# Three pairs of split weight buffers in place of four

## The chip, the cores and the metric

The kernel runs as one program on one core of a Trainium2 chip. The metric is the device time of one execution in microseconds (us), lower is better. The profile's times count from the start of the span, which is the part of the execution in which the engines work.

## The reference

Two blocks of a network run one after the other on 256 tokens of width 1024, batch 1, in float32. The first has a retention layer, a gated embedding, shared keys and values with compressed blocks, a sparse attention layer and a second gated embedding:

```python
def first_block(...):
    h = retention_layer(x, ret_norm, ret_w_in, ret_gn, ret_w_out)   # 4 heads, q k 256, v 512 wide, gate, out
    h = h + sigmoid(rmsnorm(h, g0) @ ple_w_gate0) * (p0 @ ple_w_emb0)
    shared = nsa_shared_kv(h, ...)      # rmsnorm(h) @ kv_w: 6 parts of 512; two of them compressed
    h = nsa_layer(h, ..., *shared)      # 16 heads in 4 groups: compressed, selected and window branch
    h = h + sigmoid(rmsnorm(h, g1) @ ple_w_gate1) * (p1 @ ple_w_emb1)
    return rmsnorm(h, final_norm)

def compress_blocks(a, pe, w1, w2):     # windows of 32 tokens, stride 16: 15 windows for each group
    return gelu((blocks + pe) @ w1) @ w2          # w1 is 4096 x 256

def nsa_layer(...):
    q, gate, bgate = split(rmsnorm(h, g) @ w_in)
    o = sigmoid(bgate)[0] * o_compressed + sigmoid(bgate)[1] * o_selected + sigmoid(bgate)[2] * o_window
    return h + (silu(gate) * o) @ w_out
```

With 256 tokens there are four selection blocks and the window is 512, so that the selected and the window branch are both plain causal attention. The second block takes that output as x:

```python
def second_block(x, ...):
    ua, va, za, qh, kh, vh, zb, ga, gb = split(x @ w_in)            # 9 parts of 1024
    ya = gelu(ua) * (spatial mix of layer_norm(gelu(va))) * silu(za)
    o  = softmax(q1 k1) v - lam * softmax(q2 k2) v                   # 8 heads, rotary, causal, then rms_norm
    yb = o * silu(zb)
    merged = sigmoid(ga) * (ya @ w_branch_a) + sigmoid(gb) * (yb @ w_branch_b)
    ple = sigmoid(x @ w_ple_gate) * (p @ w_ple)
    return layer_norm(2 ** 0.25 * x + merged @ w_out + ple)
```

## The kernel before

Activations stay on the chip. What streams in is the weights, 145 chunks of them, numbered 0 to 144 in the order of their first use (`plan.chunks`). A full chunk is 1 MB: four tiles of 128 rows by 512 columns (for the compression's first matrix, eight tiles by 256 columns), 2048 float32 values in each partition. Ten chunks are half as large and one is smaller still.

Each product of float32 numbers is made of three products in the type fp32r: a number is split in a high part (the number cast to fp32r) and a low part (the number less the high part), and TensorE adds high x high, high x low and low x high. For the weights this works as follows, for every chunk c:

- SyncE issues the transfer into `raw[c % 3]` (line 664). From chunk 3 on it first waits until chunk c - 3 has been split (`lo_done`, line 661).
- ScalarE makes the high part, `whi[c % SPLIT_SLOTS]`, a cast of 128 x 2048 (line 773). It waits for the transfer, and from chunk SPLIT_SLOTS on for the use of the chunk that had the buffer before (line 772).
- VectorE makes the low part, `wlo[c % SPLIT_SLOTS]`, a subtraction (line 1168). It waits for the high part.
- TensorE waits for `lo_done`, does the chunk's matmuls, and counts `chunk_used` up at the last one (lines 1703 to 1758).

Both ScalarE and VectorE have a helper `split_until(n)`, which makes all parts up to chunk n - 1 in order; each engine's whole program is written in one order, and an engine does nothing behind a wait until that wait is met. The order in which the parts are made is set by the calls of the helper:

```python
def before_block(name):
    split_until(plan.upto[name] + AHEAD)     # AHEAD = 3
    block_wait(act, name)
```

`plan.upto[name]` is the number of chunks that TensorE's order has introduced up to and with the block or the misc step `name`. So before ScalarE or VectorE waits for the result of block `name`, whose last chunk is `upto - 1`, it makes its parts of all chunks up to `upto + 2`. `before_misc` does the same for the small matmuls and transposes in between; for the transposes of a norm the look-ahead is 1 or 2 instead of 3. In some places only `split_until(... + AHEAD)` stands, ahead of a wait of another kind: ahead of the sigmoids of a gated embedding (line 878) and of the residual's adds on VectorE (line 1238), which wait for each of the two row tiles by itself.

TensorE's order is written out by hand in `tensor_order`. A block is a product with 512 columns of weights, in one to four chunks. Blocks alternate between two pairs of banks (`acc`); a block waits until its pair has been read. Two layouts occur: "nat" has the tokens in the rows of the result, with the activations as the stationary operand (lines 1718 to 1735), "tr" has them in its columns, with the weights stationary (lines 1742 to 1744). Small steps ("misc") go round four banks (`mps`): each waits until the step four before it has been read. These are the norms' transposes and all others (line 1761), the scores (lines 1841 to 1851), the transposes of the probabilities (1859, 1862) and the products with the values (1873, 1876) in the sparse attention, and the steps of the differential attention (1901, 1919 to 1921).

The order around the places that matter:

- Retention output: blocks `ret_out0`, `ret_out1` (chunks 26 to 33), then `emb0_0` and `emb0_1` (34, 35, half size), then the transposes of the norm `ple0`, then `ple0_0` and `ple0_1` (36 to 39). VectorE adds the residual (line 1242), and scales the rows (line 1209).
- `ple0_1`, `emb1_0`, `emb1_1` (40, 41), norm `kv`, then `kc`, `vc`, `ks` (42 to 47), the compression `cmp_k` (48 to 51), `kw` and `vs` (52 to 55), `cmp_v` (56 to 59), `vw` (60, 61), the first queries (62, 63) and the branch gate `nsa_b` (64; ScalarE's sigmoid is line 962, TensorE's transposes of it line 1816).
- Sparse attention, four groups of four chunks (65 to 80). In group 1 these are 69 to 72: scores of the first query tile, 69, compressed scores and scores of the second tile, 70, transposes, 71, values, transposes, 72, values. VectorE reads the scores in lines 1404 and 1418, weighs the value product in line 1445; ScalarE copies the transposes in line 994.
- The rest of `nsa_out` (81 to 86), `emb2_0` (87), norm `ple1`, `ple1_0` and `ple1_1` (88 to 91), `emb2_1` (92), norm `fin`, `ple2` (93 to 96), and the projections of the second block (97 to 120).
- Differential attention with `zb`, `ga`, `wa`, `gb` between its steps (121 to 136), then `wb0` first chunk (137), `ob` of the last heads, `wb1` first chunk (138), transposes of `ob`, gating (line 1650), `wb0` and `wb1` second chunks (139, 140), merge (line 1625) and `wo` (141 to 144).

Of the kernel before, what the change touches and what calls it, by code (L numbers as in the profile page):

```python
# [43 lines left out]


RAW_SLOTS = 3
SPLIT_SLOTS = 4
AHEAD = 3
CH = 2048
MISC = 4  # L50
# [325 lines left out]
def build(nc, w, consts, ret_consts, out):  # L376
# [5 lines left out]
    with ExitStack() as ctx:  # L382
        def sb(name, shape, dt=F32):
            return ctx.enter_context(nc.sbuf_tensor(name, shape, dt))
# [5 lines left out]
        raw = [sb(f"raw{i}", [P, CH]) for i in range(RAW_SLOTS)]  # L390
        whi = [sb(f"whi{i}", [P, CH], F32R) for i in range(SPLIT_SLOTS)]
        wlo = [sb(f"wlo{i}", [P, CH], F32R) for i in range(SPLIT_SLOTS)]

# [365 lines left out]
        def _(act):  # L759
# [3 lines left out]
            def split_until(n):  # L763

                while done[0] < min(n, len(plan.chunks)):
# [3 lines left out]
                    act.wait_ge(raw_in[c % RAW_SLOTS], 16 * (c // RAW_SLOTS + 1))  # L769
                    if c >= SPLIT_SLOTS:  # L770

                        act.wait_ge(chunk_used, plan.used_up[c - SPLIT_SLOTS])
                    nc.scalar.activation(whi[c % SPLIT_SLOTS][:, 0:size], raw[c % RAW_SLOTS][:, 0:size],  # L773
                                         ACT.Copy).then_inc(hi_done, 1)
# [378 lines left out]
        def _(dve):  # L1153
# [7 lines left out]
            def split_until(n):  # L1161

                while done[0] < min(n, len(plan.chunks)):
# [3 lines left out]
                    dve.wait_ge(hi_done, c + 1)  # L1167
                    nc.vector.tensor_tensor(wlo[c % SPLIT_SLOTS][:, 0:size], raw[c % RAW_SLOTS][:, 0:size],  # L1168
                                            whi[c % SPLIT_SLOTS][:, 0:size].bitcast(F32),
# [808 lines left out]
```

## Time and profile before

| | before |
|---|---|
| median of 3 runs | 916.99 us (916.43 to 917.31) |
| the profiled execution | 917.05 us, its span 915.0 us |
| TensorE matmuls busy | 888.4 us (97%) |
| VectorE busy | 569.2 us (62%) |
| ScalarE busy | 482.7 us (53%) |
| GpSimd busy | 37.1 us (4%) |
| moved by DMA | 154.95 MB, mean 169 GB/s |
| mean granted clock of TensorE | 0.994 |

A line of the timeline has the start in us, the duration in us, the engine, the line in the kernel, the operation, what it writes and reads with the shapes, and how many instructions are merged in it. In brackets stand the engine's idle time before it and what ended that idle time. PE is TensorE's matmul queue, DVE is VectorE, ACT is ScalarE. Matmuls overlap, so one of 390 ns can follow another by 230 ns.

### The profile page before, as it was taken

How to read it: one execution, taken by the hardware profiler on the slowest of the kernel's cores; microseconds unless marked ns; L12 is line 12 of the kernel's file. 1: busy time of each engine (PE TensorE's matmuls, PEld its weight loads, DVE VectorE, ACT ScalarE, POOL GpSimd, SP SyncE). 2: the span in 40 equal slices, each digit the busy share in tenths (PEclk: the TensorE clock that was granted, in tenths of full speed). 3: DMA queues.
4: the chain of work that ended last, by engine and by line, in shares of the span. 5: the costliest groups of instructions: out<-in, count | busy, mean ns of one | idle time of the engine just before them, and what ended most of it. 6: DMA issues, size and time to landing. Idle time of an engine off the chain costs nothing.

```text
span 915.0 us, 13668 instructions
## 1 busy us (share of the span) xinstructions
PE 888.4 (97%) x5662; PEld 786.1 (86%) x5662; DVE 569.2 (62%) x831; ACT 482.7 (53%) x709; POOL 37.1 (4%) x48
## 2 busy tenths in 40 slices
PE   5999999999999999999999999899999999999995
PEld 5998898888799988878878687788998889999994
DVE  4885565546685675544646346786559548567675
ACT  5433433327655766665757436644434448756630
POOL 1000000000100000000000002100020000000002
PEclk9999999999999999999999999999999999999998
DMA  8755544543767875324142356465556526454421
GB/s 296 269 191 182 183 134 144 196 140 113 231 200 251 278 233 165 126 93 127 58 138 75 131 185 208 158 237 184 190 177 232 184 92 212 157 185 152 132 86 46
DMA packets 81325, 154.95 MB, mean 169 GB/s; under 512 B 3761, under 2 KB 11953, under 8 KB 81265
## 3 DMA queue, kind: packets, MB, share of 16 engines
q1 hardware_dynamic: 79760, 149.23, 48.9%
q0 software_dynamic: 1504, 4.85, 1.8%
q8 instruction: 45, 0.74, 0.3%
q14 instruction: 16, 0.12, 0.0%
HBM read 153.03 MB, written 1.05 MB: 168 GB/s over the span
## 4 chain that ended last, share of the span: by engine, by line
PE 90%; ACT 3%; DVE 3%; DMA 2%; issue 1%; POOL 0%; SPq 0%; POOLq 0%; DVEq 0%; ACTq 0%
PE acc L1742 14%; PE acc L1743 13%; PE acc L1744 13%; PE acc L1733 7%; PE acc L1734 7%; PE acc L1735 7%; PE acc L1720 5%; PE acc L1718 5%; PE acc L1719 5%; PE misc L1873 2%; DMA raw<-in_ret_w_in_dram 2%; PE misc L1761 2%; PE misc L1846 2%; ACT whi L773 2%; DVE wlo L1168 1%; PE misc L1862 1%
## 5 line engine op out<-in xcount | busy, mean ns | idle before, releaser
L1168 DVE TENSOR_TENSOR wlo<-raw,whi 128x2048 fp32r<-128x2048 f32 (+1 forms) x145 | 317.4, 2204 | 166.8 <-ACT whi L773 166.2
L773 ACT ACTIVATE whi<-raw 128x2048 fp32r<-128x2048 f32 (+1 forms) x145 | 266.6, 1845 | 162.1 <-PE acc L1735 81.1
L1742 PE MATMUL acc<-xhiA,whi 128*128 128x256 f32 x576 | 165.2, 287 | 0.5 <-DVE wlo L1168 0.5
L1743 PE MATMUL acc<-xloA,whi 128*128 128x256 f32 x576 | 163.6, 284 | 0.0
L1744 PE MATMUL acc<-xhiA,wlo 128*128 128x256 f32 x576 | 163.4, 284 | 0.0
L1742 PEld LDWEIGHTS acc<-xhiA,whi 128*128 128x128 f32 x576 | 110.9, 193 | 2.9 <-issue 2.2
L1743 PEld LDWEIGHTS acc<-xloA,whi 128*128 128x128 f32 x576 | 110.9, 193 | 0.0
L1744 PEld LDWEIGHTS acc<-xhiA,wlo 128*128 128x128 f32 x576 | 110.9, 193 | 0.0
L1742 PE MATMUL acc<-xhiC,whi 128*128 128x256 f32 x320 | 93.6, 292 | 0.3 <-DVE xloC L1192 0.3
L1744 PE MATMUL acc<-xhiC,wlo 128*128 128x256 f32 x320 | 90.7, 283 | 0.0
L1743 PE MATMUL acc<-xloC,whi 128*128 128x256 f32 x320 | 90.7, 283 | 0.0
L1733 PE MATMUL acc<-whi,xhiA 128*128 128x512 f32 x160 | 64.3, 402 | 0.7 <-DVE xloA L1227 0.7
L1742 PEld LDWEIGHTS acc<-xhiC,whi 128*128 128x128 f32 x320 | 61.4, 192 | 1.5 <-issue 1.0
L1734 PE MATMUL acc<-wlo,xhiA 128*128 128x512 f32 x160 | 62.4, 390 | 0.0
L1735 PE MATMUL acc<-whi,xloA 128*128 128x512 f32 x160 | 62.4, 390 | 0.0
L1743 PEld LDWEIGHTS acc<-xloC,whi 128*128 128x128 f32 x320 | 61.5, 192 | 1.0 <-issue 1.0
L1744 PEld LDWEIGHTS acc<-xhiC,wlo 128*128 128x128 f32 x320 | 61.4, 192 | 0.0
L1742 PE MATMUL acc<-xhiB,whi 128*128 128x256 f32 x192 | 54.9, 286 | 0.9 <-DVE xloB L1227 0.9
L1743 PE MATMUL acc<-xloB,whi 128*128 128x256 f32 x192 | 54.4, 283 | 0.0
L1744 PE MATMUL acc<-xhiB,wlo 128*128 128x256 f32 x192 | 54.4, 283 | 0.0
L1720 PE MATMUL acc<-whi,xloA 128*128 128x512 f32 x128 | 49.9, 390 | 0.0
L1718 PE MATMUL acc<-whi,xhiA 128*128 128x512 f32 x128 | 49.9, 390 | 0.0
(253 smaller groups left out, 1579.6 us busy)
## 6 DMA issues: line engine op xcount, KB each, us to landing
raw<-in_w_in_dram SPq DMA_DIRECT2D x36, 1024.0 KB, 5.1
raw<-in_ret_w_in_dram SPq DMA_DIRECT2D x22, 1024.0 KB, 5.2
raw<-in_nsa_w_in_dram SPq DMA_DIRECT2D x16, 1024.0 KB, 5.2
raw<-in_kv_w_dram SPq DMA_DIRECT2D x12, 1024.0 KB, 5.3
raw<-in_ret_w_out_dram SPq DMA_DIRECT2D x8, 1024.0 KB, 5.1
raw<-in_ple_w_gate_dram SPq DMA_DIRECT2D x8, 1024.0 KB, 5.2
raw<-in_nsa_w_out_dram SPq DMA_DIRECT2D x8, 1024.0 KB, 5.1
raw<-in_cmp_w_k_dram SPq DMA_DIRECT2D x4, 1024.0 KB, 7.2
```

What stands on the lines that cost most here:

```text
L773: nc.scalar.activation(whi[c % SPLIT_SLOTS][:, 0:size], raw[c % RAW_SLOTS][:, 0:size], ACT.Copy).then_inc(hi_done, 1)
L1168: nc.vector.tensor_tensor(wlo[c % SPLIT_SLOTS][:, 0:size], raw[c % RAW_SLOTS][:, 0:size], whi[c % SPLIT_SLOTS][:, 0:size].bitcast(F32), AL ...
L1718: nc.tensor.matmul(o, xh, hi[:, j], start=first and j == 0, stop=False)
L1719: nc.tensor.matmul(o, xh, lo[:, j], start=False, stop=False)
L1720: ins = nc.tensor.matmul(o, xl, hi[:, j], start=False, stop=(j == len(ks) - 1))
L1733: nc.tensor.matmul(o, xh, hi[:, j, off:off + cols], start=start, stop=False)
L1734: nc.tensor.matmul(o, xh, lo[:, j, off:off + cols], start=False, stop=False)
L1735: ins = nc.tensor.matmul(o, xl, hi[:, j, off:off + cols], start=False, stop=stop)
L1742: nc.tensor.matmul(o, wh, xh, start=s0, stop=False, skip_group_check=True)
L1743: nc.tensor.matmul(o, wh, xl, start=False, stop=False, skip_group_check=True)
L1744: ins = nc.tensor.matmul(o, wl, xh, start=False, stop=stop, skip_group_check=True)
L1761: ins = nc.tensor.transpose(dst[:, i * P:i * P + P], s, ident)
```

## The change

The number of buffer pairs for the split weights goes from four to three. The names `whi[3]` and `wlo[3]` go away, chunk c uses the pair c % 3, and ScalarE's wait of line 772 is for the use of chunk c - 3, from chunk 3 on. The buffers for the raw weights stay three and the look-ahead stays 3. Each pair takes 16 KB in every partition.

```diff
@@ -44,7 +44,7 @@
 RAW_SLOTS = 3
-SPLIT_SLOTS = 4
+SPLIT_SLOTS = 3
 AHEAD = 3
 CH = 2048
 MISC = 4
```

The lines that it governs, unchanged themselves:

```python
whi = [sb(f"whi{i}", [P, CH], F32R) for i in range(SPLIT_SLOTS)]
wlo = [sb(f"wlo{i}", [P, CH], F32R) for i in range(SPLIT_SLOTS)]
...
if c >= SPLIT_SLOTS:
    act.wait_ge(chunk_used, plan.used_up[c - SPLIT_SLOTS])
```

## Rows read from the trace of the kernel before

**Rows 1.** The page: busy time of the engines; the groups of instructions by line.
```profile
PE 888.4 (97%) x5662; PEld 786.1 (86%) x5662; DVE 569.2 (62%) x831; ACT 482.7 (53%) x709; POOL 37.1 (4%) x48
...
L1168 DVE TENSOR_TENSOR wlo<-raw,whi 128x2048 fp32r<-128x2048 f32 (+1 forms) x145 | 317.4, 2204 | 166.8 <-ACT whi L773 166.2
```

**Rows 2.** Timeline, 190 to 221 us: the end of the retention output and its norm.
```profile
191.01 1.92 ACT L773 ACTIVATE whi<-raw 128x2048 fp32r<-128x2048 f32 x1 [3.52 <-PE acc L1735]
...
207.33 1.92 ACT L773 ACTIVATE whi<-raw 128x2048 fp32r<-128x2048 f32 x1 [4.38 <-PE acc L1735]
...
212.51 0.39 PE L1718 MATMUL acc<-whi,phi 128*128 128x512 f32 x1
...
215.34 0.75 DVE L1209 TENSOR_SCALAR arena<-h,rstd 128x1024 f32<-128x1024 f32 x1 [0.67 <-POOL rstd L681]
...
220.57 0.47 PE L1733 MATMUL acc<-whi,xhiA 128*128 128x512 f32 x1 [0.70 <-DVE xloA L1227]
```

**Rows 3.** Timeline, 237 to 251 us: the gated embedding and the norm before kc.
```profile
237.25 1.92 ACT L773 ACTIVATE whi<-raw 128x2048 fp32r<-128x2048 f32 x1 [1.71 <-PE acc L1735]
...
242.63 0.60 ACT L881 ACTIVATE arena<-acc 128x512 f32<-128x512 f32 x1 [2.12 <-PE acc L1720]
...
250.75 0.35 PE L1742 MATMUL acc<-xhiB,whi 128*128 128x256 f32 x1 [0.92 <-DVE xloB L1227]
```

**Rows 4.** Timeline of TensorE: after the norm ple1, and the norm fin.
```profile
556.93 0.47 PE L1733 MATMUL acc<-whi,xhiC 128*128 128x512 f32 x1 [0.93 <-DVE xloC L1227]
...
584.26 1.09 PE L1761 MATMUL misc<-cbuf,arena 128*128 128x128 f32 x4 [2.56 <-DVE arena L1209]
```

**Rows 5.** Windows: stretch, length, busy us of each engine, granted clock, DMA.
```profile
584.00:586.00 2.00, 1.74 (x9) 1.77 (x10) 0.11 (x1) 0.62 (x2) 0.76 (x2) 0.52 0.52 147
586.00:587.50 1.50, 1.50 (x9) 1.50 (x9) 1.16 (x3) 1.47 (x5) 0.00 (x0) 0.51 0.98 281
```

**Rows 6.** Timeline, 288 to 353 us: compression and branch gate.
```profile
288.50 6.90 DVE L1168 TENSOR_TENSOR wlo<-raw,whi 128x2048 fp32r<-128x2048 f32 x3 [4.38 <-ACT whi L773]
...
322.65 0.39 PE L1755 MATMUL acc<-whi,xloA 128*124 128x256 f32 x1 [0.69 <-DVE wlo L1168]
...
352.87 0.29 PE L1816 MATMUL misc<-cbuf,arena 48*128 48x48 f32 x2 [0.16 <-ACT arena L962]
```

**Rows 7.** Timeline, 402 to 425 us: group 1 of the sparse attention.
```profile
402.83 0.96 PE L1851 MATMUL misc<-arena 128*128 128x15 f32 x8
404.59 2.74 PE L1846 MATMUL misc<-arena 128*128 128x512 f32 x6
405.53 0.17 DVE L1404 CUSTOM_DVE_ANT_0 arena<-misc,cbuf 128x15 f32<-128x15 f32 x1
...
419.97 0.59 PE L1873 MATMUL misc<-arena 128*128 128x512 f32 x1
...
422.94 0.69 DVE L1445 TENSOR_TENSOR arena<-misc,arena 128x512 f32<-128x512 f32 x1 [1.28 <-PE misc L1876]
...
424.83 0.61 PE L1859 MATMUL misc<-cbuf,arena 128*15 128x128 f32 x4
```

**Rows 8.** Timeline, 753 to 757 us and 870 to 884 us: differential attention and tail.
```profile
753.08 4.50 DVE L1168 TENSOR_TENSOR wlo<-raw,whi 128x2048 fp32r<-128x2048 f32 x2
756.50 0.28 PE L1742 MATMUL acc<-xhiA,whi 128*128 128x256 f32 x1
...
870.96 0.60 PE L1761 MATMUL misc<-cbuf,arena 128*128 128x128 f32 x4
...
872.52 0.74 DVE L1650 SCALAR_TENSOR_TENSOR arena<-misc,small,arena 128x512 f32<-128x512 f32 x1
...
874.71 0.38 PE L1742 MATMUL acc<-xhiC,whi 128*128 128x256 f32 x1 [0.27 <-DVE xloC L1192]
...
877.97 1.40 DVE L1625 TENSOR_TENSOR arena<-arena,acc 128x512 f32<-128x512 f32 x2
...
881.83 1.22 DVE L1192 TENSOR_TENSOR xloB<-arena,xhiB 128x1024 fp32r<-128x1024 f32 x1 [1.20 <-ACT xhiB L786]
```

## The prediction

> **What bounds the kernel now.** I read the busy shares first. TensorE works in 97% of the span [rows 1], so it is the bound, and every new wait in its order adds to the time unless an old one gives way to it. The second view was the groups by line: a split on VectorE takes 2.2 us on average, 145 of them, and of VectorE's idle time 166 us ended when ScalarE's half of a split was done [rows 1]. So both engines have room, but much of it lies in front of a split, in program order, ahead of other work. The third was TensorE's order of time with its waits: after the start there are few gaps, the largest being 2.56, 0.93, 0.92, 0.70 and 0.69 us, 6.2 us for all that I show [rows 2 to 4, 6, 8]. They lie where a normalisation, a compression or a gate has to come back from ScalarE and VectorE. Those places already have no slack. The question is what the edit does there.
>
> In steady flow, ScalarE's half of chunk 33 starts at 191.01, which is when chunk 29 has been used. With 1.92 us of ScalarE and VectorE's 2.2 us [rows 1] it is full at 195.2. TensorE wants the chunk when chunk 32 is used, at 207.2 (ScalarE's next wait for it ended at 207.33) [rows 2]. The pair is full 12 us early.
>
> **The change.** It issues, removes and adds no instruction and no byte; what changes is one wait. ScalarE's half of chunk c waits for the use of chunk c-3 instead of c-4. A full chunk takes TensorE 5.3 us there (207.2 to 212.5, where the next block's first matmul is at 212.51), and somewhat more in the other layout. Chunk 33's split would start 5.3 us later, and be full some 6.6 us early. A plain split therefore stays hidden, in nearly the whole kernel. That costs nothing by itself, and no DMA is late: the transfer of c+3 still starts when VectorE has split c, and has a whole chunk's matmuls to land.
>
> The cost comes from what stands behind the split. The look-ahead stays at three, so before it waits for a block or a misc step, ScalarE first has to split the third chunk after it, and that now needs the very last chunk before the awaited step, where it needed the one before that. Both engines run in order, so everything behind is late by what is left of a chunk, plus 1.9 us of ScalarE and 2.3 of VectorE. I followed each engine's order through the kernel chunk by chunk. Where the lateness is absorbed I name the cover.
>
> *Retention, and the last block's projections.* The copies, the rotary products and the group norms come 2 to 5 us later. Their readers are a whole chunk away. 0 us; without that cover up to 4 us for each.
>
> *Norm after the retention output.* The residual's last column half stands behind the split of chunk 36. That split began at 207.33, at the end of chunk 32; now it needs chunk 33, and 212.5. The residual add behind it and the normed rows at 215.34 (second tile) move 5.3 us. TensorE had its next full chunk at 220.57, after other cover of about 2 us had run out [rows 2]. With ScalarE's extra split in the way as well, I take +4.1 us. Bounds: 3 (only the rows are late) to 5.4.
>
> *Norm before the kv projections.* Split 42 moves from 237.25 to 242.6, past both sigmoids. The second began at 242.63 when the chunk ended. TensorE already waited 0.92 us for this norm's result at 250.75 [rows 3], so nothing covers it: +5.4. The norm after the attention output (0.93 us waited, chunk 88 at 556.93) and the one before the last block (2.56 us waited) have the same two forms [rows 4]: +5.4 each. Bounds for each of the three: 4 to 6.
>
> *Compression.* The four chunks of each compression take TensorE less time each than VectorE's half of a split, so the lead is eaten. VectorE splits chunks 51 to 53 back to back from 288.50 (2.3 us each), and TensorE starts 52 the moment it is full, at 293.1; it waits 0.69 us for chunk 59 at 322.65 [rows 6]. This run begins later, since split 50 now needs chunk 47 and a copy of a key block moves in between; by the engines' orders I get 52 full at 295.1: +2.05 (an estimate). The second compression adds +2.15, by way of a copy behind split 58, which now waits for chunk 55. Bounds together: 2 to 7.
>
> *Branch gate.* It already ends TensorE's 0.16 us wait at 352.87 [rows 6]. Split 66 now stands ahead of the copy before it: 1.9 us later, +1.95. Bounds: 0 to 2.1.
>
> *Attention, four groups alike.* First, chunk 69 ends at about 403.0, where TensorE turns to the compressed scores (402.83). VectorE's first operation on these is at 405.53, behind split 72. This can't begin before 403.05 now, and is full at 403.05 + 1.9 + 2.3 = 407.25: +1.7. The fourth of the group's second scores needs this bank back; three of them take 2.74 us from 404.59, so it starts at 406.4. It would get the bank, four small operations later, at 407.8: +1.4. Second, split 74 must now wait for chunk 71, at 420.1 (TensorE turns to the weighted values at 419.97). It is full at 420.2 + 1.9 + 2.3 = 424.4, so the product of 422.94 moves 1.5 us, and with it ScalarE's copies, which free a bank for the last transpose at 424.83 [rows 7]: +1.5. In all 4 x 2.9 = 11.6. Bounds: 2 to 16.
>
> *Differential attention.* At its start VectorE splits chunks 122 and 123 at 753.08, behind an exponential of ScalarE; so 122 is full at 755.3, and wanted at 756.50 [rows 8]. ScalarE now stops for split 123 until chunk 120 is used, and is 2.1 us late; 1.2 are covered: +0.9, say 1.0 with the semaphore's way. After that ScalarE and VectorE run 2 to 4 us behind, but by their reader's order they are a chunk ahead: 0, bounds 0 to 4.
>
> *Tail.* The last head's outputs are needed at once. Split 141 had been long asked for; now it needs chunk 138, which ends at 871.1 (the transposes at 870.96), itself 1.5 us later because an earlier copy on ScalarE is late. 871.1 + 1.5 + 1.9 + 2.3 = 876.8, in place of 872.52, for the gating behind it: +4.4 at TensorE's wait of 874.71. Chunk 139 then ends at 882.2, where it ended just before 877.97; split 142 waits for it and takes 4.2; the merge at 877.97 starts at 886.5. From there to TensorE's next chunk (its operand ready at 881.83 + 1.22 = 883.05) it is 5.4 us: 891.8 instead of 883.4 [rows 8]. The tail in all: +8.3. Bounds: 4 to 10. No splits are left after it.
>
> Sum: 4.1 + 3 x 5.4 + 4.2 + 1.95 + 11.6 + 1.0 + 8.3 = 47.4 us.
>
> **The clock.** After the 2.56 us gap the granted clock was 0.52 from 584 to 586 and 0.51 on to 587.5 [rows 4, 5], the lower level (1.2 GHz), 3.3 us in all; most of that lay behind the waits of the norm anyway. Three norms get gaps of 4 to 6 us, and the tail 2.6 and 3.5. I add 0.4 us for each of the three, and 1.3 for the tail: 2.5. Bounds 0 to 13 (eight gaps over 2 us at 1.6 each, the half-speed share of those 3.3 us).
>
> The Trainium skill (page TensorE: Matmul & The Clock Gate, section HAM oscillation — how this bites in real kernels) says that a wait between bursts of matmuls can send the clock back to its lower level, so that the next burst starts slow; the trace agrees at 584.
>
> The sum is made against the profiled execution: span 915.0, 917.05 us in all. 917.05 + 47.4 + 2.5 = 967.0; the median of the runs, 916.99, lies 0.06 lower, so I say 967.
>
> **Rivals.**
> R1, nothing is seen: three pairs are enough. For it speaks that a split is full 6.5 us early still, and that over 160 us of VectorE's time are idle. It turns on one thing: if the work behind a split (residual adds, gating, bank releases) had over 5.4 us before its reader, all lateness would vanish. Against it stand TensorE's present waits at these places [rows 3, 4, 8]. Its time: 917. The Trainium skill (page Trainium Kernel Development and Optimization, section Best Practices) advises double buffering to overlap transfers with computing, and three is more than double; by that rule this one would hold.
> R2, only late splits cost: the compressions and chunk 122, 5 us, and the first norm's; the norms' other chains go on as before because the engines find time in between. 917 + 5 to 10: 925. Against it: the engines don't reorder.
> R3, the same and more: every gap over 2 us brings the lower clock for a whole 3.3 us on the path (+10), or lateness adds up from head to head in the differential attention (+4 for some): 975 to 990.
> R4, half: the bank waits in attention don't arise, since the banks come back earlier than I read, and the tail costs 4: 967 - 11.6 - 4.3 = 951.
>
> **How the numbers follow.** Forecast 0.62, with a range of its own of 958 to 975; R4 0.14; R3 0.12; R2 0.06; R1 0.06. The range of 8 in 10 takes in R4 and the lower part of R3: 946 to 979. About 0.2% (1.8 us) can be told from no change. Faster: 0.01, since nothing is removed that anyone waits for; the same 0.06; slower 0.93.
>
> **What would show it.** TensorE busy about the same in us, some 92% of the span; its idle up by some 47 us, with waits of 4 to 8 us before the norms' transposes at the four norms (releaser: VectorE's normed rows), 1.4 and 1.5 us in each attention group, and two in the tail before the gating's low half and before the first chunk of the output projection. ScalarE's idle before splits goes up, released by TensorE. Wrong would be: no gaps at the norms (R1), a stall in steady flow with the low half of a split as its releaser, or a slower matmul.

## The result and the profile after

The changed kernel takes 976.52 us, the median of four runs (974.56 to 979.8); the kernel before took 916.71 in four runs beside them (916.12 to 917.31). The ratio is 1.0656, with a 95% interval of 1.0624 to 1.0688: slower, by 59.8 us. The forecast was 967.0 (946 to 979), so the sign, the cause and the range held; its likeliest case, 958 to 975, ended 1.5 us too low, and the range held by the part that it had taken in from the rival R3. The profiled execution took 975.62 us, of which the span is 973.6, with a mean granted clock of 0.973 (0.994 before).

The page of the changed kernel: busy time by engine, the granted clock in 40 slices, the chain that ended last by engine, and the two groups of splits (busy us, mean ns of one, idle time ahead of them and what ended it).

```profile
PE 907.9 (93%) x5662; PEld 799.1 (82%) x5662; DVE 569.8 (59%) x831; ACT 486.2 (50%) x709; POOL 37.4 (4%) x48
...
PEclk9999999999899998999999998899999999999979
...
PE 83%; ACT 7%; DVE 5%; issue 3%; DMA 1%; POOL 1%; SPq 0%; POOLq 0%; DVEq 0%; ACTq 0%
...
L1168 DVE TENSOR_TENSOR wlo<-raw,whi 128x2048 fp32r<-128x2048 f32 (+1 forms) x145 | 319.3, 2206 | 298.5 <-ACT whi L773 297.8
L773 ACT ACTIVATE whi<-raw 128x2048 fp32r<-128x2048 f32 (+1 forms) x145 | 267.2, 1845 | 330.2 <-PE acc L1744 141.1
```

Beside [rows 1]: the counts are the same, and VectorE and ScalarE work as long as before. A split costs VectorE 2206 ns in place of 2204, so no split got slower. VectorE's idle time in front of its splits went from 166.8 to 298.5 us, and ScalarE's from 162.1 to 330.2, most of it ended by TensorE. The two engines do the same work and stand longer ahead of it. In the chain that ended last TensorE's share went from 90% to 83%, ScalarE's from 3% to 7%, VectorE's from 3% to 5%. TensorE's own row is the surprise: 907.9 us busy for the same 5662 matmuls, 19.5 more than before. Busy time that grows without a matmul more points to a lower clock, and the digits 8 and 7 in the row of the clock say in which slices.

TensorE's timeline after the change has these long waits (in brackets: the idle time and what ended it):

```profile
218.56 0.80 PE L1718 MATMUL acc<-whi,phi 128*128 128x512 f32 x1 [3.82 <-DVE h L1242]
225.37 0.47 PE L1733 MATMUL acc<-whi,xhiA 128*128 128x512 f32 x1 [0.70 <-DVE xloA L1227]
...
257.84 3.65 PE L1761 MATMUL misc<-cbuf,arena 128*128 128x128 f32 x16 [4.42 <-DVE arena L1209]
...
337.31 0.44 PE L1755 MATMUL acc<-whi,xloA 128*124 128x256 f32 x1 [2.18 <-DVE wlo L1168]
...
370.91 0.29 PE L1816 MATMUL misc<-cbuf,arena 48*128 48x48 f32 x2 [2.01 <-ACT arena L962]
...
431.98 1.13 PE L1846 MATMUL misc<-arena 128*128 128x512 f32 x2 [1.29 <-DVE small L1404]
...
450.90 0.66 PE L1862 MATMUL misc<-cbuf,arena 128*128 128x128 f32 x4 [0.76 <-DVE arena L1445]
452.05 0.61 PE L1859 MATMUL misc<-cbuf,arena 128*15 128x128 f32 x4 [0.49 <-ACT arena L994]
...
592.70 3.65 PE L1761 MATMUL misc<-cbuf,arena 128*128 128x128 f32 x16 [5.84 <-DVE arena L1209]
...
628.89 3.65 PE L1761 MATMUL misc<-cbuf,arena 128*128 128x128 f32 x16 [7.73 <-DVE arena L1209]
...
925.34 0.58 PE L1742 MATMUL acc<-xhiC,whi 128*128 128x256 f32 x1 [2.75 <-DVE xloC L1192]
940.31 0.47 PE L1733 MATMUL acc<-whi,xhiB 128*128 128x512 f32 x1 [3.42 <-DVE xloB L1192]
```

The releasers are normed rows, a residual add, a gate, a bank release and an operand: results that came late. Behind the opening only two kinds of wait end with a split itself, those of the compressions and of chunk 122. How a late result arises is plain on VectorE, here at the end of the retention output; it answers to [rows 2]:

```profile
212.12 1.92 ACT L773 ACTIVATE whi<-raw 128x2048 fp32r<-128x2048 f32 x1 [4.38 <-PE acc L1720]
...
214.06 2.29 DVE L1168 TENSOR_TENSOR wlo<-raw,whi 128x2048 fp32r<-128x2048 f32 x1 [5.07 <-ACT whi L773]
...
217.82 0.68 DVE L1242 TENSOR_TENSOR h<-h,acc 128x512 f32<-128x512 f32 x1
...
220.12 0.75 DVE L1209 TENSOR_SCALAR arena<-h,rstd 128x1024 f32<-128x1024 f32 x1 [0.68 <-POOL rstd L681]
```

The same instructions in the kernel before:

```profile
209.28 2.29 DVE L1168 TENSOR_TENSOR wlo<-raw,whi 128x2048 fp32r<-128x2048 f32 x1 [5.07 <-ACT whi L773]
...
213.04 0.68 DVE L1242 TENSOR_TENSOR h<-h,acc 128x512 f32<-128x512 f32 x1
```

VectorE stood idle for 5.07 us in front of this split before as well. What changed is when the wait is met: the split starts at 214.06 in place of 209.28, since ScalarE's half now waits until chunk 33 is used and not chunk 32. The last add comes at 217.82 in place of 213.04, and the normed rows at 220.12, where they came at 215.34.

A table of where the 58.6 us between the spans (973.6 less 915.0) arise. Each number is the growth, from one place to the next, of the difference between the start of a chunk in that kernel and in the kernel before, in one profiled execution each. Two experiments stand beside it, told below. (The first norm's row ends at the start of chunk 41. 0.5 of it, in all three columns, arises there, where `emb1_1` waits 0.31 us for banks that ScalarE's sigmoid of line 881 frees; by its cause it belongs to the gated embedding and so to the row below.)

| place | forecast | changed | changed, with fillers | four pairs, look-ahead 4 |
|---|---|---|---|---|
| start | 0 | -0.65 | -0.4 | -0.1 |
| norm after the retention output | 4.1 | 5.9 | 4.6 | 6.1 |
| norm before `kc` | 5.4 | 5.7 | 4.7 | 5.8 |
| compression 1 | 2.05 | 1.8 | 1.8 | -0.1 |
| compression 2 | 2.15 | 3.4 | 1.9 | -0.5 |
| branch gate | 1.95 | 5.1 | 1.8 | 1.9 |
| attention, four groups | 11.6 | 11.95 | 11.9 | 11.95 |
| norm `ple1` | 5.4 | 6.3 | 5.4 | 5.8 |
| norm `fin` | 5.4 | 6.3 | 4.5 | 6.0 |
| chunk 122 | 1.0 | 0.9 | 0.9 | 0.0 |
| differential attention | 0 | 0.25 | 0.2 | 0.25 |
| tail | 8.3 | 11.7 | 7.8 | 10.5 |
| clock, told by itself | 2.5 | in the above | | in the above |
| sum | 49.9 | 58.6 | 45.1 | 47.5 |

### The profile page after: what moved, and what is told of

Same layout as the page of the kernel before. It is cut to its first block, busy times and chain, and to the rows that moved or that the text cites. A ratio compares the mean times of both kernels' runs of the same rounds, so it can differ in the third digit from the quotient of the medians.

```text
span 973.6 us, 13669 instructions
## 1 busy us (share of the span) xinstructions
PE 907.9 (93%) x5662; PEld 799.1 (82%) x5662; DVE 569.8 (59%) x831; ACT 486.2 (50%) x709; POOL 37.4 (4%) x48
## 4 chain that ended last, share of the span: by engine, by line
PE 83%; ACT 7%; DVE 5%; issue 3%; DMA 1%; POOL 1%; SPq 0%; POOLq 0%; DVEq 0%; ACTq 0%
PE acc L1742 13%; PE acc L1743 13%; PE acc L1744 13%; PE acc L1733 7%; PE acc L1734 6%; PE acc L1735 6%; PE acc L1718 5%; PE acc L1720 5%; PE acc L1719 5%; ACT whi L773 4%; DVE wlo L1168 3%; PE misc L1761 2%; DMA raw<-in_ret_w_in_dram 1%; PE misc L1873 1%; PE misc L1841 1%
## 5 line engine op out<-in xcount | busy, mean ns | idle before, releaser
L1168 DVE TENSOR_TENSOR wlo<-raw,whi 128x2048 fp32r<-128x2048 f32 (+1 forms) x145 | 319.3, 2206 | 298.5 <-ACT whi L773 297.8
L773 ACT ACTIVATE whi<-raw 128x2048 fp32r<-128x2048 f32 (+1 forms) x145 | 267.2, 1845 | 330.2 <-PE acc L1744 141.1
L1733 PE MATMUL acc<-whi,xhiA 128*128 128x512 f32 x160 | 64.7, 405 | 0.7 <-DVE xloA L1227 0.7
L1735 PE MATMUL acc<-whi,xloA 128*128 128x512 f32 x160 | 62.6, 391 | 0.0
L1761 PE MATMUL misc<-cbuf,arena 128*128 128x128 f32 x184 | 31.1, 325 | 27.5 <-DVE arena L1209 27.3
L1761 PEld LDWEIGHTS misc<-cbuf,arena 128*128 128x128 f32 x184 | 26.9, 171 | 29.8 <-issue 29.1
```

The costliest lines, as they stand in the source:

```text
L1733: nc.tensor.matmul(o, xh, hi[:, j, off:off + cols], start=start, stop=False)
L1735: ins = nc.tensor.matmul(o, xl, hi[:, j, off:off + cols], start=False, stop=stop)
L1761: ins = nc.tensor.transpose(dst[:, i * P:i * P + P], s, ident)
```

## The experiments

The theory, T1: the pair that is missing hurts by the order of the programs. A split that is asked for `AHEAD` chunks early waits for the use of the chunk `SPLIT_SLOTS` before it; with both at three, that is the last chunk of the very block whose result stands behind the split. Rivals: T2, the pairs themselves are too few to keep TensorE fed; T3, the raw buffers come free later, and the transfers arrive late; and for the 10 us beyond the waits, that the clock is not what costs them.

Each ratio below is to the kernel before, measured beside the experiment; its medians there are 916.2 to 916.8.

**Three pairs, look-ahead 2** (`s3_a2`) and **four pairs, look-ahead 2** (`s4_a2`).

```diff
-AHEAD = 3
+AHEAD = 2
```

> Three pairs, look-ahead 2 in place of 3. T1 (order: the cost is that a split whose wait is for the last chunk of the awaited block stands ahead of the reads of that block) expects nearly the time of the kernel before, 917 to 930 us, say 924: the split ahead of a read then needs the last chunk but one again, and only the places with short chunks (the compressions, chunk 122) still have too little lead. T2 (shortage: three pairs hold too little, whatever the order) expects 976 us or more, since splits are asked for later still. T3 (transfers start late) expects 970 to 980.

> Four pairs as before, look-ahead 2. T1 expects the kernel before or a little less, 910 to 918 us, say 914: the splits ahead of the norms' reads then wait for a chunk that has long been used, so that a part of the 5 us of gaps at the four norms goes. T2 expects 917 to 925, since pairs are filled later. T3 expects 917 to 920.

Measured: 930.08 (929.33 to 931.01) with three pairs, ratio 1.0150 (1.0135 to 1.0165), and 929.99 (929.1 to 930.25) with four, ratio 1.0147 (1.0132 to 1.0162). One constant gives 46 of the 60 us back with three pairs, and at look-ahead 2 a fourth pair makes no difference that can be told. T2 falls. But the times that T1 had named, 924 and 914, were missed by 6 and by 16: a shorter look-ahead has a price of its own. Of the 12.7 in the span 5.7 are at the compressions, where the lead is eaten, and 7.5 at chunk 121. VectorE's and TensorE's timelines of four pairs, look-ahead 2:

```profile
758.79 0.16 DVE L1567 TENSOR_TENSOR small<-small 128x1 f32<-128x1 f32 x1 [11.27 <-ACT small L1087]
758.99 0.15 DVE L1568 TENSOR_SCALAR small<-small 128x1 f32<-128x1 f32 x1
759.17 2.29 DVE L1168 TENSOR_TENSOR wlo<-raw,whi 128x2048 fp32r<-128x2048 f32 x1
```

```profile
761.57 0.55 PE L1742 MATMUL acc<-xhiA,whi 128*128 128x256 f32 x1 [4.76 <-issue]
```

VectorE waits 11.27 us for an exponential of ScalarE, and the low half of chunk 121 stands behind that wait. With look-ahead 3 it was made before it. "issue" as the releaser is a place where the page does not name the cause; VectorE's split that ends at 761.46 does.

**Three pairs, look-ahead 2, and chunk 121 split before that wait** (`s3_a2_lam`). One line is added on VectorE:

```diff
+                split_until(plan.upto["vh1"] + 1)
                 dve.wait_ge(lam_done, 1)
```

> Three pairs, look-ahead 2, and VectorE makes its half of chunk 121 before it waits for the exponential of lambda instead of behind it. The order theory puts 6.6 us of the 13 that look-ahead 2 still costs on that one place (TensorE waits 4.8 us for chunk 121 and runs half of it slowly), so 930 - 6.6 = 923.5 us, 921 to 926. If the 13 us were a general lack of lead, nothing would change: 929 to 931.

Measured: 923.71 (921.86 to 924.39), ratio 1.0072 (1.0054 to 1.0089). The wait of 4.76 is gone, and three pairs now cost 0.7%. Of what is left, 6.3 in the span, 5.6 are at the compressions.

**Four pairs, look-ahead 4** (`s4_a4`). The reverse test: no buffer is taken away, but look-ahead and pairs are equal again.

```diff
-AHEAD = 3
+AHEAD = 4
```

> Four pairs as before, look-ahead 4 in place of 3: as many buffers as before, but the split ahead of a read again needs the last chunk of the awaited block. T1 expects the slowdown of the change nearly whole: 955 to 977 us, say 968, less than 976 only where the second chunk of lead helps (compressions, chunk 122). T2 expects 910 to 917, since nothing is taken away and pairs are filled earlier. T3 expects 917.

Measured: 966.48 (963.42 to 969.36), ratio 1.0546 (1.0517 to 1.0576). The kernel before, with nothing removed, loses 50 us at the same places with the same waits (last column of the table). What it doesn't show are the compressions (-0.6 for both) and chunk 122 (0). These are what the missing pair adds at look-ahead 3, 4.6 us without the clock. From its timeline of TensorE:

```profile
219.09 0.79 PE L1718 MATMUL acc<-whi,phi 128*128 128x512 f32 x1 [3.82 <-DVE h L1242]
...
258.55 3.65 PE L1761 MATMUL misc<-cbuf,arena 128*128 128x128 f32 x16 [4.43 <-DVE arena L1209]
...
365.88 0.30 PE L1816 MATMUL misc<-cbuf,arena 48*128 48x48 f32 x2 [2.01 <-ACT arena L962]
...
584.48 3.44 PE L1761 MATMUL misc<-cbuf,arena 128*128 128x128 f32 x16 [5.84 <-DVE arena L1209]
620.17 3.65 PE L1761 MATMUL misc<-cbuf,arena 128*128 128x128 f32 x16 [7.74 <-DVE arena L1209]
```

Waits of 3.82, 4.43, 2.01, 5.84 and 7.74, where the changed kernel has 3.82, 4.42, 2.01, 5.84 and 7.73.

**Five raw buffers** (`s3_raw5`), against T3.

```diff
-RAW_SLOTS = 3
-SPLIT_SLOTS = 4
+RAW_SLOTS = 5
+SPLIT_SLOTS = 3
```

> Three pairs, look-ahead 3 as in the changed kernel, but five raw buffers in place of three, so that every weight transfer may start two chunks earlier than now. It tells the order of the programs (T1) from the transfers (T3: with three pairs the raw buffers come free later and the weights arrive late). T1: the first halves wait for a pair, not for a raw buffer, and a second half still frees its raw buffer in the same order; time 974 to 979, the same waits of TensorE at the same places (3.8 before the second gated embedding, 4.4, 5.8 and 7.7 at the three norms, 2.8 and 3.4 in the tail), only the opening of the kernel may move by up to 1. T3: the raw buffers matter, and at least 5 of the 57 are given back: 970 or less.

Measured: 977.54 (975.79 to 979.85), ratio 1.0664 (1.0646 to 1.0683). Two more raw buffers change nothing that can be told; TensorE's waits are 3.82, 4.43, 5.84, 7.73, 2.75 and 3.72. T3 falls.

**One part of the order at a time.** Three kernels have three pairs, look-ahead 3, and look-ahead 2 in one part: `s3_norm` at the residual adds and the gated embeddings, `s3_attn` in the sparse attention, `s3_tail` from the differential attention on (`LATE` is 2 there). One edit of each stands for the rest:

```diff
-            split_until(plan.upto["ret_out1"] + AHEAD)
+            split_until(plan.upto["ret_out1"] + AHEAD - 1)
...
-                    before_misc("PV", g, qt)
+                    before_misc("PV", g, qt, ahead=AHEAD - 1)
...
-                        before_misc("obT", j)
+                        before_misc("obT", j, ahead=LATE)
```

> Three pairs, look-ahead 3, but 2 at the residual adds and at the gated embeddings alone (ScalarE and VectorE). T1 expects the gaps at the four norms to go, and only these: 5.5 + 6.2 + 6.3 + 6.3 = 24.2 us by the traces, so 976.5 - 24.2 = 952 us (948 to 958). T2 and T3 expect 973 to 978.

> The changed kernel with look-ahead 2 in place of 3 at the scores, the transposes and the value products of the sparse attention alone. The order theory expects the two waits of each group to go (1.55 + 1.43 us, four times, 11.9 us by the traces) and the rest to stay: 976.5 - 11.9 = 964.6 us, 962 to 968. The shortage theory expects no gain, 974 to 979.

> The changed kernel with look-ahead 2 from the differential attention to the end alone. The order theory expects the tail's 11.7 us and 0.24 before it to go, its 0.9 us at chunk 122 to stay: 964.5 us, 962 to 968. The shortage theory expects no gain, 974 to 979.

Measured: 954.94 (954.36 to 955.63), ratio 1.0420 (1.0403 to 1.0438); 962.15 (960.85 to 963.27), 1.0493 (1.0477 to 1.0509); 964.63 (960.35 to 966.05), 1.0513 (1.0486 to 1.0540). Each gives back its own part and leaves the others, but for what the clock moves (up to 2.4 at one place). By the starts of the chunks the four norms go from 24.1 to 3.0, the four groups of the attention from 11.95 to 0, the tail from 11.7 to 0.0. So the parts of the table add up as a forecast needs it, and each is caused where it stands. The medians give 21.6, 14.4 and 11.9 back. The 14.4 is 2.4 more than the attention lost; its trace has these 2.4 in the tail (9.4 in place of 11.7), where nothing was edited and the clock is the higher one behind the wait of 2.75 us. The changed kernel's own runs lie 5.2 apart, so this is no finding.

**The changed kernel with filler matmuls in eight of its waits** (`s3_warm`). Matmuls of the identity by the identity go into banks that are overwritten afterwards, 126 calls that the trace shows as 252 instructions: 16 to 60 at a place, sized to end before the result is there, since they only fill the time in which TensorE would wait.

```diff
+            def warm(n, after=None, bank_of=None):
+                ...
+                for _ in range(n):
+                    nc.tensor.matmul(bank_of[:, 0:P], ident, ident, start=True, stop=True)
...
+                if (name, i) == ("emb0_1", 0):
+                    k = plan.misc_no[("norm", "ple0", 0)]
+                    warm(14, misc_names[k - MISC], mps[k % MISC])
```

> The changed kernel with extra matmuls of the identity (128x128, result never read) on TensorE in eight of its waits: before the last half-size chunk ahead of the first norm (14), before the transposes of the other three norms (18, 24, 30), before the last chunk of the second compression (8), before the branch gate's transposes (8), inside chunk 139 (11) and before chunk 141 (13), each lot somewhat shorter than the wait it lies in. If the lower clock after the waits costs about 10 us, as the traces say, the time falls by 7 to 10, to 966 to 970 us, the granted clock goes above 0.99 and the runs lie closer together than the 5 us of the changed kernel. If the clock costs what the forecast had, 2.5 us, it falls to 974; if the waits alone explain it all, 976 to 980, since the extra matmuls can only be in the way.

Measured: 962.61 (962.2 to 962.88), ratio 1.0498 (1.0483 to 1.0514). With 252 matmuls more the kernel is 13.9 us faster, and its runs lie 0.7 us apart in place of 5.2. No wait for a result can get shorter by it, so what is recovered is the clock. Windows of the changed kernel, which begin with the transposes of the norms at 257.84 and 592.70 (columns: stretch, length, busy us of PE, PEld, DVE, ACT, POOL, granted clock, DMA share, GB/s):

```profile
257.80:261.50 3.70, 3.66 (x17) 3.69 (x18) 1.58 (x4) 3.54 (x9) 1.33 (x3) 0.50 0.50 142
592.70:596.40 3.70, 3.70 (x17) 3.70 (x18) 1.63 (x4) 3.54 (x10) 3.16 (x6) 0.50 0.77 286
```

The first of these places with fillers, as a window and as TensorE's timeline (lines below the edit are 20 higher in this kernel, and 1700 is the filler):

```profile
252.20:259.00 6.80, 6.15 (x53) 5.71 (x51) 3.42 (x7) 5.25 (x11) 3.71 (x6) 1.00 0.56 193
```

```profile
252.21 4.18 PE L1700 MATMUL misc<-cbuf 128*128 128x128 f32 x36
256.70 1.97 PE L1781 MATMUL misc<-cbuf,arena 128*128 128x128 f32 x16 [0.32 <-DVE arena L1209]
259.65 0.36 PE L1762 MATMUL acc<-xhiB,whi 128*128 128x256 f32 x1 [0.98 <-DVE xloB L1227]
```

The same 16 transposes take 1.97 us in place of 3.65, at a granted clock of 1.00 (2.4 GHz) in place of 0.50 (1.2 GHz). The difference between the table's columns gives the clock's price by place: 1.3 and 1.0 at the first two norms, 1.5 at the second compression, 3.3 at the branch gate, 0.9 and 1.8 at the last two norms, 3.9 in the tail; 0 in the attention, whose waits of 1.3 and less have 1.00 behind them. In the norm `fin` 0.6 of the 1.8 is no loss of the change: there the kernel before runs at the lower clock itself [rows 5].

**Four pairs, look-ahead 2 at the norms only** (`s4_mix`), which the traces pointed to as a gain of up to 0.6, and then `s4_mix2` and `s3_norm2`. `s4_mix` has the five edits of `s3_norm` on the kernel before.

> Four pairs and look-ahead 3, as the kernel before, with look-ahead 2 only at the residual adds and the gated embeddings (five calls, on ScalarE and on VectorE). If the order of the programs decides (T1), then fewer halves of a chunk stand ahead of the norms' own work: in the traces of four pairs with look-ahead 2 everywhere the last norm was 0.6 and the one at 557 was 0.3 earlier than in the kernel before, the one at 250 was 0.4 later, and nothing else of that kernel's 13 lost is at these places. T1: 916.0 to 917.0, a gain of 0 to 0.6 that is hardly to be told from none. Rival (look-ahead is always worth having, a shorter one costs wherever it is used): 919 or more.

Measured: 920.66 (919.5 to 921.99), ratio 1.0044 (1.0031 to 1.0056): slower by 3.8, a miss, and the rival's number. ScalarE's timeline of this kernel:

```profile
246.12 3.70 ACT L773 ACTIVATE whi<-raw 128x2048 fp32r<-128x2048 f32 x2
249.72 1.06 ACT L871 ACTIVATE gains<-acc 128x512 f32<-128x512 f32 x2
250.68 3.03 ACT L818 ACTIVATE xhiB<-misc,cbuf 128x256 fp32r<-128x256 f32 x8
```

The split that the adds no longer ask for is made up by the next caller, the copy of an embedding, which still looks 3 ahead; and behind that stand the high halves of the norm's operand. The other two kernels look 2 ahead at the copies too, with four pairs and with three:

```diff
-                before_block(f"emb{n}_{i}")
+                split_until(plan.upto[f"emb{n}_{i}"] + AHEAD - 1)
+                block_wait(act, f"emb{n}_{i}")
```

> The run before this with four pairs and the shorter look-ahead at five calls took 920.7, 3.8 more than the kernel before. Its trace shows ScalarE making two first halves in a row (3.70) at 246.12, ahead of the copy of the embedding and of the norm's high halves, where the kernel before has one (1.90): the half that the residual add no longer asks for is made up at the copy of the embedding, which still looks 3 ahead and stands in front of the norm. This kernel looks 2 ahead at those copies too (a sixth call). If that is the cause, the norms at 250 and 557 lose their 1.80 and 1.49 and the 1.49 of the low clock behind the first of them: 915.9 to 917.4. Rival (a shorter look-ahead costs by itself wherever it is used): 920 to 921 again, or more.

> Three pairs, look-ahead 3 in general, 2 at the residual adds and the gated embeddings (954.9 in the earlier run) and now at the copies of the embeddings too. The earlier run kept 1.8 at the norm at 250 and 1.8 at the one at 557. By the same cause as above, the half that is made up ahead of the norm on ScalarE, these go down to the 0.4 and -0.3 of the kernels that look 2 ahead everywhere: 951 to 952. Rival: 954 to 956 as before.

Measured: 916.81 (916.54 to 917.69) for `s4_mix2`, ratio 1.0002 (0.9993 to 1.0011), the same as the kernel before; and 949.41 (949.22 to 951.07) for `s3_norm2`, ratio 1.0361 (1.0346 to 1.0377), 5.5 less than `s3_norm` and 1.6 below what was expected. By the starts of the chunks (6.0 in the span) 3.2 are at the two norms, as the theory has it. Of the rest 1.6 are at the branch gate, behind whose wait of 2.01 us, the same in both, the granted clock is 0.88 over 14 us in place of 0.76. The other 1.3 are at the first compression, where `s3_norm` waits 1.36 us for chunk 52; what ends that wait the trace does not name, and it stays open. ScalarE's timeline of `s4_mix2` at that place (its line 872 is 871 of the kernel before):

```profile
245.73 1.90 ACT L773 ACTIVATE whi<-raw 128x2048 fp32r<-128x2048 f32 x1
247.54 1.06 ACT L872 ACTIVATE gains<-acc 128x512 f32<-128x512 f32 x2
248.49 1.57 ACT L818 ACTIVATE xhiB<-misc,cbuf 128x256 fp32r<-128x256 f32 x4
```

One split again, and the norm goes on at 248.49 instead of 250.68. So the rival, that a shorter look-ahead costs wherever it is used, falls too: it costs where a split is moved behind a wait or in front of an urgent result. No version beat the kernel before.

## Why the prediction was right, and what it had too small

*The mechanism* was right: an unchanged look-ahead over fewer pairs puts a wait for TensorE's last chunk ahead of in-order work. Two experiments show it from both sides, by taking the look-ahead down (930.08) and by taking it up without touching the pairs (966.48).

*Plain splits stay hidden*: right. In the steady stretches no wait of TensorE ends with a split; the lead of chunk 33, forecast at 6.6 us, is 6.4. The transfers are not late (`s3_raw5`).

*Norm after the retention output*, 4.1: the size was right, the place was not. Without the clock it costs 4.1 up to the start of chunk 40 (4.6 with the wait at chunk 41). I had followed the normed rows. What TensorE waits for is 3.82 us ahead of `emb0_1`, for its pair of banks, which the last residual add of line 1242 frees. Both hang on the same late split. A step that follows a result should also follow the buffer that the reader gives back.

*The three other norms*, 5.4 each: 5.2 (4.7 and the 0.5 at chunk 41), 5.4 and 5.1 without the clock; the last is the table's 4.5 and the 0.6 that the kernel before loses there by its own clock. The places and releasers are as forecast. A wait's length in a trace isn't its price: ahead of the transposes of `ple1` and `fin` the waits are 5.84 and 7.73, but 0.84 and 2.56 of these were there before. The forecast's list of the largest gaps leaves out that 0.84, at 554.06.

*Compressions*, 2.05 and 2.15: 1.8 and 1.9. *Branch gate*, 1.95: 1.8. *Chunk 122*, 1.0: 0.9. *Attention*, 4 x 2.9: 4 x 2.99, as 1.55 and 1.43 in each group for the forecast's 1.4 and 1.5. *Tail*, 8.3: 7.8. In all the waits come to 45.1 in place of 47.4, start and all.

*The clock* is the term that was mis-sized: 2.5 forecast, 13.5 measured as the difference of the spans with and without fillers (973.6 less 960.1), 13.9 by the medians. That is just beyond the end of its bounds, 13, which were eight gaps over 2 us at 1.6 each; the trace has eight such waits behind the opening (3.82, 4.42, 2.18, 2.01, 5.84, 7.73, 2.75 and 3.42). Two parts of the reasoning failed. First, I let the low clock lie behind the waits of the norm, as it mostly did in [rows 4, 5]. With waits of 4 to 8 us the norm's chain is TensorE's own: 16 transposes at half speed are 1.7 us more, on the path, and the next chunk begins slow as well (chunk 42 takes 6.56 us, before 5.99). Second, I counted the norms and the tail only. The second compression and the branch gate have waits of 2.18 and 2.01, and lose 1.5 and 3.3 by it, the gate more than its wait. R3 had this mechanism ("the lower clock for a whole 3.3 us on the path, +10") and time, 975 to 990; the measured 976.5 lies in it. The waits went as the forecast had them, the clock as R3 had it. One sign failed with the clock: TensorE's idle time went up by 39.1 and not by 47, and its busy time by 19.5. Some of the slow matmuls lie where it waited before: the wait of 0.92 behind the transposes at 250.75 [rows 3] is gone.

*The other rivals.* R1 (917) and R2 (925) are excluded by the waits at the norms. R4 (951) is excluded: the bank waits in the attention are there. Three pairs do overlap transfers, splits and matmuls, and take 923.7 or 976.5 us by the place of the waits in the program. The Trainium skill (page Trainium Kernel Development and Optimization, section Best Practices) advises to double-buffer for that overlap; by that rule the time would have been 917, and the measured one is 976.5.

## What to carry to other kernels

Where producers run ahead by a fixed number of items on in-order engines, buffers minus look-ahead is the number that counts: at 1 a producer that is about to read the consumer's result first waits for the last item but one of that result, which is done while the last one runs (ScalarE's wait for chunk 32, met at 207.33 [rows 2]); at 0 it waits for the last item itself, and everything behind it in program order is late by that. At 2 (four pairs, look-ahead 2) nothing more was gained. So a buffer is taken away together with one step of look-ahead, and then each wait of another kind is checked for splits that have moved behind it (here one, worth 6.4 us), and each urgent result for splits that have moved ahead of it. A wait of over 2 us on TensorE is to be priced with the slow matmuls that may follow it, here about 30% on top of the waits.

## What the runs showed of the hardware

The clock's fall isn't set by the length of the wait alone. The changed kernel and the one with four pairs and look-ahead 4 have the same wait of 2.01 us ahead of the branch gate's transposes. A window of each, from that wait's end:

```profile
370.90:385.00 14.10, 14.09 (x78) 12.71 (x78) 3.56 (x28) 8.21 (x27) 0.00 (x0) 0.76 0.38 138
```

```profile
365.80:380.00 14.20, 12.83 (x81) 10.62 (x82) 6.76 (x40) 7.96 (x27) 0.00 (x0) 1.00 0.38 137
```

The mean granted clock is 0.76 in the one and 1.00 in the other; the first loses 5.1 us there, the second 1.9. The wait of 2.56 us ahead of the norm `fin` is another case. Behind it the kernel before has the lower clock, and the one with four pairs and look-ahead 2 has not, and is 0.6 us faster there:

```profile
584.20:588.20 4.00, 3.94 (x19) 3.89 (x20) 1.86 (x5) 2.79 (x8) 0.56 (x2) 0.59 0.79 247
```

```profile
589.90:593.90 4.00, 3.22 (x22) 2.82 (x23) 1.66 (x4) 3.25 (x6) 0.58 (x2) 1.00 0.76 254
```

Nor is it set by the instructions around it. Up to the sparse attention `s3_attn` is the changed kernel without a difference, and has the same wait ahead of `emb0_1` (3.81 us). A window of each behind that wait, the changed kernel first:

```profile
218.50:226.50 8.00, 7.24 (x33) 5.98 (x34) 3.75 (x8) 6.60 (x14) 0.63 (x2) 0.82 0.30 116
```

```profile
219.00:227.00 8.00, 7.33 (x28) 5.82 (x28) 2.53 (x7) 5.37 (x11) 0.63 (x2) 0.65 0.30 116
```

Up to the start of chunk 40 the place costs 5.4 us in the one execution and 6.7 in the other. Both kernels also do the same from the differential attention on, and have the same wait of 2.75 us in the tail. The windows behind it:

```profile
925.30:933.00 7.70, 7.66 (x41) 7.66 (x42) 0.12 (x1) 1.92 (x1) 0.00 (x0) 0.60 0.31 119
```

```profile
915.10:922.80 7.70, 7.68 (x64) 7.68 (x65) 2.49 (x2) 1.92 (x1) 0.00 (x0) 1.00 0.31 119
```

So what the clock adds at one place moves by over 1 us between executions of the same instructions. This may be why the changed kernel's runs lie 5.2 us apart; with fillers they lie 0.7 apart.

The Trainium skill (page TensorE: Matmul & The Clock Gate, section HAM oscillation — how this bites in real kernels) tells of waits for transfers between bursts of matmuls that bring the lower clock again and again. Here the waits are for results of other engines, and the trace agrees: the granted clock is 0.50 from 257.8 and from 592.7, behind waits of 4.42 and 5.84 us.

Cheap matmuls into a free bank were enough to keep the clock: 252 of them, 13.9 us back. In the kernel before, whose clock is 0.994, there is little to get by it; this was not tried.
